# Gates, branches and output projection of the sample tokens in two column halves, the second half moved into the expert stage

## The chip, the cores and the metric

One core of one Trainium2 chip runs the whole program. The engines are PE (TensorE, matrix products), DVE (VectorE), ACT (ScalarE), POOL (GpSimd, here it only issues gathers) and SP (SyncE, here it only issues weight loads). The metric is the device time of one execution in microseconds.

## The reference

Two groups of tokens, 128 prompt tokens and 512 sample tokens, go through two layers (D is 1024). One layer, cut to what matters here:

```python
h = rms_norm(x, norm1) * (1.0 + sc1) + sh1          # shift, scale, gate: silu(cond) @ w_ada
proj = h @ w_in                                     # 3072 gate columns, then the inputs of A, B, C
ya = chunk_gating_mlp(za, ...)                      # branch A
yb = hyena_branch(zb, ...)                          # branch B: long convolution over all tokens
yc = latent_attention(...) @ w_uv                   # branch C: the sample reads all its own keys and the context
ga, gb, gc = split(sigmoid(gates), 3)
merged = ga * (ya @ w_branch_a) + gb * (yb @ w_branch_b) + gc * (yc @ w_branch_c)
x = x + g1 * (merged @ w_out)
h2 = rms_norm(x, norm2) * (1.0 + sc2) + sh2
q = h2 @ peer_wq                                    # 8 heads x 2 x 128
idx, g = the 16 best of 128 * 128 pairs of sub-keys per head     # 8 * 16 = 128 experts a token
a = gelu(dot(peer_u[idx], h2))                      # one row of 1024 per token and expert
x = x + g2 * sum over experts of g * a * peer_v[idx]
```

All four lines from `ga, gb, gc` to `h2` work on each token by itself: they don't mix tokens.

## The kernel before

All data are fp32 with channels on the partitions and tokens along the free axis, so a weight block is the left factor of a matmul and 512 sample tokens are one row of 512 columns. Two tracks share every engine. The **mixing track** does, instance by instance, conditioning (`A`), mixing of the prompt (`P`), queries and key search (`Q`), and mixing of the sample (`S`). The **expert track** goes in slots: one slot is one expert of 128 tokens. In a slot POOL gathers 128 rows of `peer_u` (0.52 MB, line 2182) and 128 rows of `peer_v`; DVE multiplies the u rows with the tokens and sums (`dot_product`, line 2074, a pass over 128x1024). In the prompt's expert stage DVE also adds the v rows to the sum (line 2116), 18 slots later. In the sample's expert stage PE does that: DVE makes a diagonal matrix (line 2149) and PE multiplies it with the v rows, two matmuls of 128x512 a slot (line 1318).

The prompt's expert stage has 174 slots (20 for the choice of experts, 128 dots, and a tail), and the sample's has 512 and a tail (four tiles of 128 tokens). `cuts()` writes a table that says up to which place of the mixing track an engine must have come when it enters a slot, and `weave()` makes each engine's instruction order from it. Every engine runs in that order. `mix_share()` spreads an instance over slots in proportion to `cost()`.

- In the prompt's expert stage the mixing track does the sample's mixing: projections, the inputs of A and B, attention in 16 steps, then 24 gate turns (line 860, left factor from w_in, 8 matmuls of 128x512 each) with 24 branch products (line 860 as well), 8 output turns, norm 2 (line 805). DVE multiplies branch by gate in line 1862 and adds in line 1866; ACT makes the next input `h_s` in line 1383.
- Then the queries of tile 0 run alone up to the first key search, and the sample's expert stage begins.
- In that stage, mixing does the queries of tiles 1 to 3 (slots 17 to 156; PE line 867), next layer's conditioning (157 to 252), prompt mixing (253 to 472) and prompt queries (473 to 508). In the last layer only the final norms are left.

Weights come through SP's queue into a ring of three places of 1 MB, in one fixed order; a load waits until PE has used the load three places back. A gate turn uses half of a 1 MB load (256 of the 3072 gate columns), so a load serves two turns of all 512 tokens. A key search of one turn (`best_keys`, lines 1895 to 1906) is the part of the queries that falls to DVE.

The places that the change touches, in before:

```python
        return [(2 * n, 2 * n + 1) for n in range(4)] if self.sample else [(0,), (1,)]
QUERIES_S = [[Inst("Q", l, True, tiles) for tiles in ((0,), (1, 2, 3))] for l in range(LAYERS)]
                for n in range(4 * two):
                    yield PLACE[i, ("out", n)]
        over(q1, 17, 156)
```

Of the kernel before, what the change touches and what calls it, by code (L numbers as in the profile page):

```python
# [5 lines left out]
ALU = mybir.AluOpType  # L6
# [5 lines left out]
P = 128  # L12
D = 1024
# [54 lines left out]
class Inst:  # L68


    def __init__(self, kind, l, sample=False, tiles=(0,)):
        self.kind, self.l, self.sample, self.tiles = kind, l, sample, tiles
        self.W, self.NT, self.BPT = (SAMPLE, STILES, 1) if self.sample else (PROMPT, 1, 2)
        self.g = 0 if self.sample else 1
# [5 lines left out]
    def gate_groups(self):  # L80

        return [(2 * n, 2 * n + 1) for n in range(4)] if self.sample else [(0,), (1,)]

    def query_turns(self):
# [8 lines left out]
QUERIES_S = [[Inst("Q", l, True, tiles) for tiles in ((0,), (1, 2, 3))] for l in range(LAYERS)]  # L93
# [3 lines left out]
                   for i in [ADAS[l], PROMPTS[l], QUERIES_P[l], SAMPLES[l]] + QUERIES_S[l]] + LASTS  # L97
# [15 lines left out]
def step_turns(m):  # L113
# [15 lines left out]
    return turns  # L129


def turn_order(i):
# [17 lines left out]
    if kind == "Q":  # L150
# [16 lines left out]
        return o  # L167
    s = kind == "S"
# [23 lines left out]
    for group in i.gate_groups():  # L192
        for b in range(3):
            for t in group:
                ring(("gate", b, t))
                if not s:
                    o.append((("gateb", b, t), None))
                ring(("branch", b, t))
    if not s:
        ring(("mt", 0), ("mt", 1))  # L200
    ring(*[("out", n) for n in range(4 * two)], "norm2")
# [3 lines left out]
RING = {"A": (0, 1, 2), "I": (0, 1, 2, 3, 4, 6, 7), "P": (0, 1, 2), "S": (0, 1, 2, 3, 4, 6, 7), "F": (0, 1, 2),  # L205
        "Q": (0, 1, 2)}


def turn_table():

    turns, places, used, at = {}, {}, [0] * 8, 0
    for i in INSTS:
        ring = 0
        for name, bank in turn_order(i):
# [4 lines left out]
            if bank == "ring":  # L219
                bank = RING[i.kind][ring % len(RING[i.kind])]  # L220
                ring += 1
# [8 lines left out]
def bank_uses(last, bank):  # L230

    return max([n + 1 for (i, _), (b, n) in TURN.items() if b == bank and INSTS.index(i) <= INSTS.index(last)],
               default=0)


def chunk_order(i):
# [11 lines left out]
    if i.kind == "Q":  # L248
# [3 lines left out]
        return o  # L252
    take(("QK", 0), ("full", ("qk", i.NT - 1)))
# [13 lines left out]
    for n, group in enumerate(i.gate_groups()):  # L267
        last = group[-1]
        for b in range(3):
            if i.sample:  # L270
                take(("gate", b, n), ("full", ("gate", b, last)))
            else:
                take(("gate", b, n, 0), ("half", ("gate", b, n, 0)))
                take(("gate", b, n, 1), ("full", ("gate", b, last)))
            if b == 0:
                take(("ab", n), ("full", ("branch", 1, last)), 2)
        take(("c", n), ("full", ("branch", 2, last)))
    for n in range(D // CW):
        take(("out", n), ("full", ("out", n * two + two - 1)))
# [6 lines left out]
def chunk_table():  # L286
# [3 lines left out]
    for i in [i for i in INSTS if i.kind in "APSQ"]:  # L290
# [19 lines left out]
def cost(i, name):  # L310
# [3 lines left out]
    if not i.sample and kind in ("gate", "branch"):  # L314
# [6 lines left out]
def mix_share(i):  # L321

    names = [name for name, _ in turn_order(i) if (i, name) in PLACE]
    if i.sample:
# [11 lines left out]
SPREAD = 0.97  # L336
FIRST_SLOT = -PARTS
# [14 lines left out]
def cuts():  # L352
# [3 lines left out]
    for l in range(LAYERS):  # L356
        s, (q0, q1) = SAMPLES[l], QUERIES_S[l]
        for place, share in mix_share(s):
            o.append((slot_of(l, False, min(PROMPT_SLOTS, int(share / SPREAD * PROMPT_SLOTS))), place))
# [10 lines left out]
        over(q1, 17, 156)  # L370
        if l + 1 < LAYERS:
            ada, pr, qp = ADAS[l + 1], PROMPTS[l + 1], QUERIES_P[l + 1]
            over(ada, 157, 252)
            over(pr, 253, 472)
            over(qp, 473, 508)
            end = PLACE[SAMPLES[l + 1], "begin"] - 1
        else:
            for n, i in enumerate(LASTS):
                at = 160 if i.l == STILES else max(184, (i.l + 1) * EXPERTS + M_LAG + 12)
# [68 lines left out]
def build(nc, x_prompt, x_sample, cache_ckv, cache_kpe, c, c_ctx, w_ada, b_ada, norm1, norm2, w_in,  # L448
# [4 lines left out]
    with ExitStack() as ctx:  # L453
# [46 lines left out]
        WORK = 17792  # L500
# [18 lines left out]
        for v, w, n, zc0, kt0, u0, cv0, free, past_keys in ((at_s, SAMPLE, STILES, 0, 2048, 3328, 4352, 7424, PAST),  # L519
# [4 lines left out]
            v.sq2 = view(u0, KC, w)  # L524
            v.hy, v.y_f = view(free, n, 3 * B_W), view(free + n * 768, n, 2 * B_W)
# [9 lines left out]
        v.gate_s, v.gate_y = view(11520, 3, SAMPLE), view(13056, 2, SAMPLE)  # L535
        v.pq_rows, v.pqs, v.rep = view(13184, 2, BANK), view(14208, 2, BANK), view(15232, 4, P)
# [12 lines left out]

        def at(i):  # L550
            return at_s if i.sample else at_p
# [7 lines left out]
        SCRATCH = 896  # L559
        diag = view(9216 + SCRATCH, TOPK, P)  # L560
        y_tok = view(9216 + SCRATCH + TOPK * P, D)
# [81 lines left out]
        merged_ready = signal("merged_ready", P=1, S=1)  # L643
# [15 lines left out]
        def _(sp):  # L659
# [67 lines left out]
            def weights(i):  # L727
# [5 lines left out]
                if i.kind == "Q":  # L733
# [3 lines left out]
                    return  # L737
                for half in range(2):
# [1562 lines left out]
```

## Time and profile before

| what | value |
|---|---|
| median of 3 runs | 4953.66 us (4944.09 to 4954.17) |
| the profiled execution | 4948.02 us |
| its span | 4946.0 us |
| mean granted clock of TensorE | 0.934 |
| busy: PE, DVE, POOL, ACT | 3994.3, 3194.8, 2500.0, 599.3 us |
| moved by DMA | 1579.52 MB, mean 319 GB/s |

The profile is one execution; its time is the span and 2.0 us around it. Stretches below are given by their start and end in the span. In layer 0 the prompt's expert stage with the sample's mixing lies from 342.75 to 1033.6 us (projections and A, B until 535, attention until 696, gates and outputs after that), and the sample's expert stage starts with the dot at 1082.3 us. A row "PE x16" of line 860 counts each fp32 matmul twice, so x16 is one gate turn.

### The profile page before, as it was taken

To read this page: it belongs to the slowest core of one execution; us is meant where nothing else is said; L and a number is where in the kernel's file an instruction comes from. 1 tells how busy PE (TensorE), PEld (TensorE's weight loads), DVE (VectorE), ACT (ScalarE), POOL (GpSimd) and SP (SyncE) were. 2 spreads that over 40 slices of the span, in tenths; PEclk is the share of its full clock that TensorE was granted. 3 is DMA by queue.
4 is the path that set the end of the run, shared out by engine and by line. 5 is a ranking of instruction groups with operands and counts; after the bars stand their busy time and mean duration, and the time that the engine had idled before them with its cause. 6 is when DMAs were issued, how large, how long until landed. Compare 5 with 4: busy or idle time off the path is not lost.

```text
span 4946.0 us, 36846 instructions
## 1 busy us (share of the span) xinstructions
PE 3994.3 (81%) x10767; PEld 1782.0 (36%) x10767; DVE 3194.8 (65%) x7509; ACT 599.3 (12%) x1238; POOL 2500.0 (51%) x2570
## 2 busy tenths in 40 slices
PE   8889789767888886887778888987588777777777
PEld 4554343333333333443333433433233332322223
DVE  0256887647776556765655779774877876676763
ACT  1131330010000001010100314101000100000000
POOL 0002346415665555665555143551366677677774
PEclk9899899888999999999999989998799999999999
DMA  8545779848999999999999366994799999999997
GB/s 275 172 145 193 240 257 335 291 153 319 386 360 376 395 393 367 382 396 386 382 371 360 105 243 220 330 332 139 270 378 376 349 400 409 383 408 387 403 409 299
DMA packets 549494, 1579.52 MB, mean 319 GB/s; under 512 B 51168, under 2 KB 176688, under 8 KB 548018
## 3 DMA queue, kind: packets, MB, share of 16 engines
q0 software_dynamic: 368640, 1342.34, 71.7%
q1 hardware_dynamic: 180082, 234.68, 13.9%
q8 instruction: 90, 1.47, 0.1%
q14 instruction: 106, 0.87, 0.1%
q10 hardware_dynamic: 576, 0.16, 0.0%
HBM read 1574.21 MB, written 2.79 MB: 319 GB/s over the span
## 4 chain that ended last, share of the span: by engine, by line
DMA 34%; PE 22%; DVE 21%; POOL 12%; issue 7%; DVEq 2%; SPq 1%; ACT 1%; PEldq 0%; PEld 0%; ACTq 0%; POOLq 0%
DMA rows<-in_peer_u_dram,idx 30%; POOL rows L2182 10%; DVE rows L2074 8%; PE ps L1318 5%; PE ps L860 5%; PE ps L867 3%; DVE work L2116 3%; DMA rows<-in_peer_v_dram,idx 2%; PE ps L830 2%; POOL work L2182 2%; PE ps L900 1%; SPq L694 1%; DMA work<-in_peer_v_dram,idx 1%; DVEq L1951 1%; DVE work L1898 1%
## 5 line engine op out<-in xcount | busy, mean ns | idle before, releaser
L2182 POOL DMA_INDIRECT rows<-in_peer_u_dram,idx x1280 | 1250.4, 977 | 1526.8 <-DVE dots L2074 654.3
L2074 DVE CUSTOM_DVE_ANT_0 rows<-rows,ps 128x1024 f32<-128x1024 f32 x1024 | 1247.1, 1219 | 884.4 <-DMA rows<-in_peer_u_dram,idx 867.4
L1318 PE MATMUL ps<-rows,work 128*128 128x512 f32 x2736 | 1315.6, 614 | 283.9 <-DMA rows<-in_peer_v_dram,idx 256.5
L2182 POOL DMA_INDIRECT rows<-in_peer_v_dram,idx x940 | 928.0, 987 | 743.2 <-DVE work L2116 394.9
L1318 PEld LDWEIGHTS ps<-rows,work 128*128 128x128 f32 x2736 | 497.5, 194 | 1029.4 <-issue 814.8
L1318 PE MATMUL ps<-work 128*128 128x512 f32 x1360 | 659.2, 614 | 142.9 <-DMA work<-in_peer_v_dram,idx 127.2
L860 PE MATMUL ps<-h_s,ring 128*128 128x512 f32 x1024 | 473.0, 619 | 41.9 <-DVE work L1862 37.7
L1318 PEld LDWEIGHTS ps<-work 128*128 128x128 f32 x1360 | 246.0, 193 | 507.0 <-issue 391.8
L2074 DVE CUSTOM_DVE_ANT_0 rows<-rows,work 128x1024 f32<-128x1024 f32 x256 | 312.1, 1224 | 150.3 <-DMA rows<-in_peer_u_dram,idx 144.9
L2182 POOL DMA_INDIRECT work<-in_peer_v_dram,idx x340 | 320.8, 944 | 147.3 <-issue 87.5
L2149 DVE TENSOR_SCALAR work<-cst,acts,g_w 128x128 f32<-128x128 f32 x1024 | 366.9, 360 | 41.4 <-PE ps L1318 18.6
L2116 DVE SCALAR_TENSOR_TENSOR work<-rows,acts,work 128x1024 f32<-128x1024 f32 x254 | 325.5, 1282 | 15.7 <-DMA rows<-in_peer_v_dram,idx 11.0
L860 PEld LDWEIGHTS ps<-h_s,ring 128*128 128x128 f32 x1024 | 201.4, 199 | 307.5 <-issue 302.7
L860 PE MATMUL ps<-work,ring 128*128 128x512 f32 (+1 forms) x768 | 265.4, 498 | 38.6 <-DVE work L1866 30.4
L867 PE MATMUL ps<-ring,h_s 128*128 128x512 f32 x512 | 237.9, 611 | 21.4 <-ACT h_s L1383 21.4
L860 PEld LDWEIGHTS ps<-work,ring 128*128 128x128 f32 x768 | 128.8, 195 | 169.4 <-issue 123.6
L1630 ACT ACTIVATE acts<-dots 128x16 f32<-128x16 f32 x80 | 17.3, 216 | 1387.8 <-DVEq L2077 1387.7
L867 PE MATMUL ps<-ring,h_p 128*128 128x512 f32 x320 | 153.2, 628 | 23.8 <-DMA ring<-in_w_in_dram 18.0
L830 PE MATMUL ps<-ring,cond_t 128*2 128x256 f32 x768 | 169.8, 379 | 1.3 <-DVE work L1899 1.3
L867 PEld LDWEIGHTS ps<-ring,h_s 128*128 128x128 f32 x512 | 99.4, 197 | 143.2 <-issue 120.1
L1223 PE MATMUL ps<-turned,work 128*128 128x128 f32 x320 | 47.7, 297 | 88.6 <-ACT work L1502 74.2
L2074 DVE DVE_READ_ACCUMULATOR2_ANT dots<- 128x1 f32 x1280 | 105.3, 82 | 0.0
(292 smaller groups left out, 3213.4 us busy)
## 6 DMA issues: line engine op xcount, KB each, us to landing
ring<-in_w_in_dram SPq DMA_DIRECT2D x68, 1024.0 KB, 11.8
ring<-in_w_ada_dram SPq DMA_DIRECT2D x48, 1024.0 KB, 14.2
ring<-in_peer_wq_dram SPq DMA_DIRECT2D x48, 1024.0 KB, 5.2
rows<-in_peer_u_dram,idx POOLq DMA_INDIRECT x1280, 7.3
ring<-in_w_out_dram SPq DMA_DIRECT2D x16, 1024.0 KB, 13.3
rows<-in_peer_v_dram,idx POOLq DMA_INDIRECT x940, 7.3
ring<-in_tables_dram SPq DMA_DIRECT2D x10, 1024.0 KB, 8.0
ring<-in_w_in_dram SPq DMA_DIRECT2D x8, 832.0 KB, 9.3
```

What stands on the lines that cost most here:

```text
L694: sp.dma_start(dst, src).then_inc(params_in, 16)
L830: mm = pe.matmul(a[0:2, 0:CW], cond_t[:, 0:2, k], w[:, k, :], start=k == 0, stop=k == KC - 1)
L860: mm = pe.matmul(a[:, b * i.W:(b + 1) * i.W], w[:, at_w + k, c0 + b * P:c0 + (b + 1) * P], rhs[k], start=k == 0, stop=k == n_rhs - 1)
L867: mm = pe.matmul(a[:, :], lhs[4 * half + k], w[:, k, :], start=half + k == 0, stop=half * k == 3)
L900: mm = pe.matmul(a[:, 0:QK], v.h[:, k, j * P:(j + 1) * P], wqk[k // 4][:, k % 4, :], start=k == 0, stop=k == KC - 1)
L1318: mm = pe.matmul(y_acc[:, cols], diag[:, e % TOPK, :], v_row_of(t, e)[:, cols], start=e == 0, stop=e == EXPERTS - 1)
L1898: dve.match_replace(rep[k], value[:, 0:8], src[k], -3.0e38)
L1951: dve.drain()
L2074: dve.tensor_tensor_reduce(rows[:, s, :], rows[:, s, :], tok, 1.0, 0.0, ALU.mult, ALU.add, dots[:, e:e + 1]).then_inc(rows_u_free, 1)
L2116: ins = dve.scalar_tensor_tensor(y_p, v_row_of(t, e), acts[:, e:e + 1], y_p, ALU.mult, ALU.add)
L2149: dve.tensor_scalar(diag[:, e % TOPK, :], ident, acts[:, e:e + 1], g_w[:, t % 2, e:e + 1], ALU.mult, ALU.mult).then_inc(diag_ready, 1)
L2182: pool.indirect_dma_start(to, None, table, bass.IndirectOffsetOnAxis(ap=idx[:, t % 2, e:e + 1], axis=0)).then_inc(came, 16)
```

## The change

The sample's gates, branches, output projection and norm 2 become instances of their own (`G`), one for tiles 0 and 1 and one for tiles 2 and 3. Each is 256 columns wide and puts two blocks of 128 output channels in one bank, so it has 12 gate turns of 16 matmuls of 128x256 where the whole had 24 turns of 8 matmuls of 128x512; 4 output turns; and a norm of 256 columns. The first (`g0`) stands where all of it stood, at the end of the prompt's expert stage. The second (`g1`) stands in the sample's expert stage at slots 37 to 170, and loads the same weights a second time: per layer 12 loads of 1 MB of w_in, 4 MB of w_out and 4 MB of the branch weights, 20 MiB, that is 20.97 MB. The queries follow the halves: pass `q0` holds tiles 0 and 1 (before only tile 0), pass `q1` tiles 2 and 3 (before 1 to 3). In the prompt's expert stage the sample's mixing is given 0.77 of the slots and `g0` the rest. The rest of the diff makes signal counts follow and gives the second half buffers.

```diff
-QUERIES_S = [[Inst("Q", l, True, tiles) for tiles in ((0,), (1, 2, 3))] for l in range(LAYERS)]
+HALVES = ((0, 1), (2, 3))
+GATES_S = [[Inst("G", l, True, tiles) for tiles in HALVES] for l in range(LAYERS)]
+QUERIES_S = [[Inst("Q", l, True, tiles) for tiles in HALVES] for l in range(LAYERS)]
...
+        if kind == "G":
+
+            self.W, self.NT, self.BPT = len(tiles) * P, len(tiles), 2
...
+def gates_order(i, ring, o):
+    for group in i.gate_groups():
+        for b in range(3):
+            for t in group:
+                ring(("gate", b, t))
+                if not i.sample:
+                    o.append((("gateb", b, t), None))
+                ring(("branch", b, t))
+    if not i.sample:
+        ring(("mt", 0), ("mt", 1))
+    ring(*[("out", n) for n in range(D // CW)], "norm2")
...
+def ring_of(i):
+
+    return (0, 1, 2) if i.kind == "G" and i.first else RING[i.kind]
...
+            if i.sample:
+                take(("gate", b, n), ("full", ("gate", b, last)))
...
+S_SHARE = 0.77
...
-        s, (q0, q1) = SAMPLES[l], QUERIES_S[l]
-        for place, share in mix_share(s):
-            o.append((slot_of(l, False, min(PROMPT_SLOTS, int(share / SPREAD * PROMPT_SLOTS))), place))
+        s, (g0, g1), (q0, q1) = SAMPLES[l], GATES_S[l], QUERIES_S[l]
+        for i, lo, hi in ((s, 0, S_SHARE), (g0, S_SHARE, 1)):
+            for place, share in mix_share(i):
+                share = (lo + share * (hi - lo)) / SPREAD
+                o.append((slot_of(l, False, min(PROMPT_SLOTS, int(share * PROMPT_SLOTS))), place))
...
-        steps = [(FIRST_SLOT, PLACE[q0, ("pqt", 0, 1)]), (FIRST_SLOT + 2, PLACE[q0, ("pqb", 0, 2)]),
-                 (FIRST_SLOT + 4, PLACE[q0, ("key", 0, 1)]), (0, PLACE[q0, ("pqt", 0, 2)]),
-                 (4, PLACE[q0, ("pqb", 0, 3)]), (9, PLACE[q0, ("key", 0, 2)]), (16, PLACE[q0, ("key", 0, 3)])]
+        steps = [(FIRST_SLOT, PLACE[q0, ("pqb", 1, 0)]), (FIRST_SLOT + 2, PLACE[q0, ("pqt", 1, 0)]),
+                 (FIRST_SLOT + 3, PLACE[q0, ("pqb", 0, 1)]), (-1, PLACE[q0, ("key", 0, 1)]),
+                 (6, PLACE[q0, ("pqb", 0, 2)]), (10, PLACE[q0, ("key", 0, 2)]), (20, PLACE[q0, ("pqb", 0, 3)]),
+                 (30, PLACE[q0, ("key", 0, 3)]), (36, PLACE[q0, ("key", 1, 3)])]
...
-        over(q1, 17, 156)
+        over(g1, 37, 170)
+        over(q1, 171, 240)
...
-            over(ada, 157, 252)
-            over(pr, 253, 472)
-            over(qp, 473, 508)
+            over(ada, 241, 316)
+            over(pr, 317, 480)
+            over(qp, 481, 508)
...
+                for i in (PROMPTS[l], QUERIES_P[l], SAMPLES[l], GATES_S[l][0], QUERIES_S[l][0], GATES_S[l][1],
+                          QUERIES_S[l][1]):
                     weights(i)
...
-                for n in range(4 * two):
+                for n in range(D // CW):
...
-                            pe.wait_ge(h_ready.sem, h_ready.after(SAMPLES[l], 2 * KC))
+                                pe.wait_ge(bank_taken[b], bank_uses(GATES_S[l][0], b))
+                        if j % 2 == 0:
+                            pe.wait_ge(h_ready.sem, h_ready.after(GATES_S[l][j // 2], KC))
```

How the order of the instructions changes is shown at three places. On PE at the end of attention (line 1134, the last of branch C) before has a gate turn of 8 and a branch product of 2 or 4 matmuls of 128x512, 24 times:

```order
L1134 MATMUL ps<-work,uv 64x512 x2
L860 MATMUL ps<-h_s,ring 128x512 x8
L860 MATMUL ps<-work,ring 128x512 x2
L860 MATMUL ps<-h_s,ring 128x512 x8
L860 MATMUL ps<-work,ring 128x512 x2
L860 MATMUL ps<-h_s,ring 128x512 x8
```

and the changed kernel, at the same place, where line 860 has become line 927, 12 times:

```order
L1207 MATMUL ps<-work,uv 64x512 x2
L927 MATMUL ps<-h_s,ring 128x256 x16
L927 MATMUL ps<-work,ring 128x256 x4
L927 MATMUL ps<-h_s,ring 128x256 x16
L927 MATMUL ps<-work,ring 128x256 x4
L927 MATMUL ps<-h_s,ring 128x256 x16
```

Each turn keeps its columns in sum (8 x 512 and 16 x 256); there are half as many turns here, and each needs a load of its own. The other half of them stands on PE in the sample's expert stage. There before has the expert's matmuls (line 1318) with the query matmuls (line 867, 4 in a piece) between them:

```order
L1318 MATMUL ps<-work 128x512 x4
L1318 MATMUL ps<-rows,work 128x512 x6
L1215 MATMUL ps<-cst,work 128x128 x4
L1318 MATMUL ps<-rows,work 128x512 x2
L867 MATMUL ps<-ring,h_s 128x512 x4
```

and the changed kernel (line 1318 is now 1393) a little later in that stage:

```order
L927 MATMUL ps<-h_s,ring 128x256 x16
L1393 MATMUL ps<-work 128x512 x4
L1393 MATMUL ps<-rows,work 128x512 x4
L927 MATMUL ps<-work,ring 128x256 x4
L1393 MATMUL ps<-rows,work 128x512 x4
L1393 MATMUL ps<-work 128x512 x4
L927 MATMUL ps<-h_s,ring 128x256 x16
```

A gate turn of 16 matmuls now stands in one piece between the matmuls of two experts. On DVE, the gate stage of before has three dots (line 2074) and three v sums (line 2116) between two branch products (line 1862), from the first product to the last:

```order
L1862 TENSOR_TENSOR work<-work,ps 128x512
L2074 ISA rows,dots<-rows,work 128x1024
L2074 ISA dots 128x1
L2116 SCALAR_TENSOR_TENSOR work<-rows,acts,work 128x1024
L2074 ISA rows,dots<-rows,work 128x1024
L2074 ISA dots 128x1
L2116 SCALAR_TENSOR_TENSOR work<-rows,acts,work 128x1024
L2074 ISA rows,dots<-rows,work 128x1024
L2074 ISA dots 128x1
L2116 SCALAR_TENSOR_TENSOR work<-rows,acts,work 128x1024
L1862 TENSOR_TENSOR work<-work,ps 128x512
```

and the changed kernel (dots in line 2167, v sums in 2209, products in 1954) has this from its third product to its fifth:

```order
L1954 TENSOR_TENSOR work<-work,ps 128x512
L1957 TENSOR_TENSOR work<-work 128x512
L2167 ISA rows,dots<-rows,work 128x1024
L2167 ISA dots 128x1
L2209 SCALAR_TENSOR_TENSOR work<-rows,acts,work 128x1024
L2167 ISA rows,dots<-rows,work 128x1024
L2167 ISA dots 128x1
L2209 SCALAR_TENSOR_TENSOR work<-rows,acts,work 128x1024
L1954 TENSOR_TENSOR work<-work,ps 128x512
L2209 SCALAR_TENSOR_TENSOR work<-rows,acts,work 128x1024 x2
L1954 TENSOR_TENSOR work<-work,ps 128x512
```

After that product there are no dots of the prompt left, only v sums. Counted over the whole order, the first branch product of the sample's gates stands behind 69 dots and 50 v sums of the prompt's 128 in before, and behind 121 dots and 102 v sums in the changed kernel: 52 dots and 52 v sums have moved ahead of the gates, 31 of each ahead of the first softmax step of attention and 21 into attention.

## Rows read from the trace of the kernel before

**Rows 1.** The page: the chain that ended last, by engine.

```profile
DMA 34%; PE 22%; DVE 21%; POOL 12%; issue 7%; DVEq 2%; SPq 1%; ACT 1%; PEldq 0%; PEld 0%; ACTq 0%; POOLq 0%
```

**Rows 2.** Windows, prompt's stage: us; PE, PEld, DVE, ACT, POOL busy; clock; DMA share; GB/s.

```profile
342.75:535.00 192.25, 170.30 (x458) 83.93 (x458) 136.39 (x282) 33.85 (x66) 57.85 (x51) 0.89 0.57 199
535.00:696.00 161.00, 134.10 (x443) 64.92 (x441) 142.31 (x279) 76.15 (x226) 64.46 (x66) 0.91 0.65 210
696.00:1033.60 337.60, 297.94 (x665) 128.69 (x664) 212.26 (x268) 33.36 (x49) 158.48 (x140) 0.94 0.81 284
```

**Rows 3.** Same view, sample's expert stage of layer 0, then of layer 1.

```profile
1185.50:1590.80 405.30, 343.83 (x896) 151.77 (x896) 292.68 (x888) 27.13 (x46) 256.08 (x271) 0.96 0.97 372
1590.80:1825.80 235.00, 195.17 (x568) 71.89 (x568) 127.90 (x287) 12.63 (x29) 131.77 (x141) 1.00 1.04 395
3982.50:4166.30 183.80, 138.68 (x309) 51.00 (x308) 130.58 (x295) 11.90 (x18) 133.47 (x141) 1.00 1.02 407
```

**Rows 4.** PE's timeline, gate stage: start, us, line, what, count, idle before.

```profile
696.00 7.13 PE L860 MATMUL ps<-h_s,ring 128*128 128x512 f32 x16
...
809.52 7.11 PE L860 MATMUL ps<-h_s,ring 128*128 128x512 f32 x16
...
999.10 27.63 PE L860 MATMUL ps<-work,ring 128*128 128x512 f32 x64
...
1044.32 9.80 PE L867 MATMUL ps<-ring,h_s 128*128 128x512 f32 x16 [10.72 <-ACT h_s L1383]
```

**Rows 5.** DMA from 696 to 1033.6: loads, KB each, median us to landing.

```profile
ring<-in_w_in_dram SPq DMA_DIRECT2D x10, 1024.0 KB, 14.1
...
ring<-in_peer_wq_dram SPq DMA_DIRECT2D x3, 1024.0 KB, 5.0
```

**Rows 6.** PE's timeline in the projections: one turn of 256 columns.

```profile
350.31 3.62 PE L908 MATMUL ps<-ring,h_s 128*128 128x256 f32 x16
```

**Rows 7.** DVE's timeline in attention: one dot, one v sum, the next step.

```profile
548.76 1.23 DVE L2074 CUSTOM_DVE_ANT_0 rows<-rows,work 128x1024 f32<-128x1024 f32 x1
...
549.91 1.28 DVE L2116 SCALAR_TENSOR_TENSOR work<-rows,acts,work 128x1024 f32<-128x1024 f32 x1
551.28 0.16 DVE L1937 TENSOR_TENSOR stat<-stat 128x1 f32<-128x1 f32 x1
```

**Rows 8.** DVE by line, 340 to 1050: busy, mean ns, idle before, releaser.

```profile
L1789 DVE TENSOR_SCALAR work<-ps,par 128x512 f32<-128x512 f32 x6 | 4.9, 809 | 8.3 <-PE ps L860 8.3
...
L1818 DVE TENSOR_TENSOR work<-work 128x256 f32<-128x256 f32 x4 | 1.7, 426 | 9.8 <-ACT work L1454 9.4 <-issue 0.5
...
L1810 DVE TENSOR_TENSOR work<-work,ps 128x512 f32<-128x512 f32 x2 | 1.4, 689 | 10.2 <-PE ps L939 10.2
```

**Rows 9.** Same columns, dots alone: 340 to 535, 535 to 696, 696 to 1034.

```profile
L2074 DVE CUSTOM_DVE_ANT_0 rows<-rows,work 128x1024 f32<-128x1024 f32 x31 | 37.3, 1222 | 10.3 <-DMA rows<-in_peer_u_dram,idx 9.2 <-issue 0.2
...
L2074 DVE CUSTOM_DVE_ANT_0 rows<-rows,work 128x1024 f32<-128x1024 f32 x34 | 41.6, 1222 | 1.5 <-DMA rows<-in_peer_u_dram,idx 1.1 <-issue 0.3
...
L2074 DVE CUSTOM_DVE_ANT_0 rows<-rows,work 128x1024 f32<-128x1024 f32 x63 | 77.3, 1226 | 63.4 <-DMA rows<-in_peer_u_dram,idx 62.2
```

**Rows 10.** DVE's timeline, start of the sample's expert stage: one key search.

```profile
1083.44 0.89 DVE L1895 MAX8 work<-ps 128x8 f32<-128x128 f32 x4
...
1088.93 1.22 DVE L2074 CUSTOM_DVE_ANT_0 rows<-rows,ps 128x1024 f32<-128x1024 f32 x1
```

**Rows 11.** DMA queues, packets, MB: 1590.8 to 1825.8, then 3982.5 to 4166.3.

```profile
q0 software_dynamic: 20266, 73.80, 80.6%
q1 hardware_dynamic: 18952, 18.89, 22.9%
...
q0 software_dynamic: 20206, 73.59, 100.8%
q1 hardware_dynamic: 288, 1.05, 1.4%
```

**Rows 12.** PE's timeline in the sample's expert stage: three experts' matmuls.

```profile
2154.10 5.31 PE L1318 MATMUL ps<-rows,work 128*128 128x512 f32 x12
```

More of the change, by code:

```diff
@@ L80, in gate_groups, with nth_norm @@
     def gate_groups(self):
-        return [(2 * n, 2 * n + 1) for n in range(4)] if self.sample else [(0,), (1,)]
+        return [(n,) for n in range(4 if self.sample else 2)]
+    def nth_norm(self, which):
+        return 0 if self.kind == "G" else which
     def query_turns(self):
@@ L191, in turn_order @@
         ring(*[(name, c) for name in "qKSTV" for c in range(2)], ("Y", 0))
[L192 to L198, printed above, removed]
     if not s:
-        ring(("mt", 0), ("mt", 1))
-    ring(*[("out", n) for n in range(4 * two)], "norm2")
-    return o
-RING = {"A": (0, 1, 2), "I": (0, 1, 2, 3, 4, 6, 7), "P": (0, 1, 2), "S": (0, 1, 2, 3, 4, 6, 7), "F": (0, 1, 2),
-        "Q": (0, 1, 2)}
+        gates_order(i, ring, o)
+    return o
+RING = {"A": (0, 1, 2), "I": (0, 1, 2, 3, 4, 6, 7), "P": (0, 1, 2), "S": (0, 1, 2, 3, 4, 6, 7), "G": (0, 1, 2, 3, 4, 6, 7),
+        "F": (0, 1, 2), "Q": (0, 1, 2)}
+def ring_of(i):
+    return (0, 1, 2) if i.kind == "G" and i.first else RING[i.kind]
 def turn_table():
@@ L233, in bank_uses, with gates_chunks @@
                default=0)
+def gates_chunks(i, take):
+    for n, group in enumerate(i.gate_groups()):
+        last = group[-1]
+        for b in range(3):
+            if i.sample:
+                take(("gate", b, n), ("full", ("gate", b, last)))
+            else:
+                take(("gate", b, n, 0), ("half", ("gate", b, n, 0)))
+                take(("gate", b, n, 1), ("full", ("gate", b, last)))
+            if b == 0:
+                take(("ab", n), ("full", ("branch", 1, last)), 2)
+        take(("c", n), ("full", ("branch", 2, last)))
+    for n in range(D // CW):
+        take(("out", n), ("full", ("out", n)))
 def chunk_order(i):
@@ L266, in chunk_order @@
         take("DFT", ("full", ("idft", 0)), 2)
[L267 to L279, printed above, removed]
+        gates_chunks(i, take)
     return o
@@ L313, in cost @@
     w = 4 if i.sample else 2
-    if not i.sample and kind in ("gate", "branch"):
+    if i.kind != "S" and kind in ("gate", "branch"):
         w = {"gate": 2, "branch": 4}[kind]
@@ L1274, in mixing @@
                         yield from queries(i)
+                    elif i.kind == "G":
+                        yield from gates(i)
                     else:
@@ L1465, in mix @@
                     a = full(i, ("gate", b, t))
-                    if r >= 3:
-                        act.wait_ge(*taken_at(i, ("branch",) + slots[r - 3]))
-                    took(act.activation(v.gate_s[:, r % 3, :], a[:, :], ACT.Sigmoid), i, ("gate", b, t))
+                    ring = len(v.gate_s)
+                    if r >= ring:
+                        act.wait_ge(*taken_at(i, ("branch",) + slots[r - ring]))
+                    took(act.activation(v.gate_s[r % ring], a[:, :], ACT.Sigmoid), i, ("gate", b, t))
                 if not i.sample:
```

137 lines of the change are left out of this document (95 added, 42 removed).

## The prediction

> **What bounds the kernel now.** I read the chain that ended last first: DMA has the largest share, 34%, with PE and DVE at 22 and 21% [rows 1]. No engine binds throughout, so the stretches have to be looked at one by one.
>
> In the prompt's expert stage the DMA is not full: 0.57 and 0.65 of the time up to the end of attention, 0.81 in the gate stage [rows 2]. PE leads in the projections (170.3 of 192.3 us) and in the gate stage (297.9 of 337.6), DVE in attention (142.3 of 161.0). In the sample's expert stage the DMA share is 0.97 to 1.04 at 372 to 407 GB/s [rows 3]: gathers and weights together fill the DMA there, and PE (83 to 85% in layer 0) and DVE wait for rows. So the change takes PE work from a stage that PE sets and gives it, with a second load of the weights, to a stage that the DMA sets. Whether that pays depends on what the weights cost there, and on what happens to the prompt's dots and v sums that now lie under the gates.
>
> **The change part by part, per layer.** I make the sum for one layer and double it: the order is the same in both.
>
> *1. The gate stage halves.* Twelve turns with their branch products take 809.52 − 696.00 = 113.5 us; the output turns run from 999.10 for 27.6 us, and from their end to 1033.6 norm 2 takes 6.9 [rows 4]. That row is the second half of the projection's matmuls (x64 of x128). After: 12 turns of as many columns (113.5), half of the projection (27.6), 3.5 of norm 2, and some 4 for the waits for the last merge and the last output. That is 149 in place of 337.6, **−188**. Late weights could take some of it back: the same loads (five for a group of three turns, four groups, and four of w_out) must now come in half the time. A group of five is used in 28.4 us (113.5 / 4), and a load may start when the one three back has been used, so it has the time of two loads' use, on average 2 × 5.7 = 11.4 us. Landing took 14.1 us in the gate stage and 5.0 right behind it [rows 5]. At 5.0 nothing is late; at 14.1 each of 20 loads is 2.7 late, 54 us. Only 7 dots and 26 v sums stay beside these turns by the order, most of them in the first half, so I take a value near the quiet end: +4.
>
> *2. The prompt's dots and v sums move ahead.* 52 dots and 52 v sums leave the gate stage. A dot with a v sum occupies DVE for 551.28 − 548.76 = 2.52 us in attention [rows 7], so they bring 52 × 2.52 = 131. DVE is at 142 of 161 us in attention, so there they lengthen the stage in full. Ahead of attention DVE idles for 192.3 − 136.4 = 55.9 us [rows 2], and three of its waits there, for PE and ACT, are long enough to take in a dot: 8.3 + 9.8 + 10.2 = 28 [rows 8]. The moved dots wait for their rows in turn: 10.3 / 31 = 0.33 us each ahead of attention (31 of them, 10), 1.5 / 34 each within (21, 1) [rows 9]. Together 131 − 28 + 11 = **+114**. Bounds: all idle time ahead of attention filled and no wait, 131 − 56 = 75; nothing filled and each dot waiting as in the gate stage, 63.4 / 63 = 1.0 us, 183. I take 114, because the nearest rows (same stage, same instructions) give 0.33 and not 1.0.
>
> *3. Norm, h and first queries.* PE waits 10.72 us for the last `h_s` before the queries [rows 4]; ACT and DVE have half the columns to do there: **−5** (bounds 0 and −8).
>
> *4. Two more key searches* fall into the first slots, since q0 has two tiles. One takes 1088.93 − 1083.44 = 5.5 us of DVE [rows 10], ahead of a dot on whose row place the next gather waits. The rest of the stage has two fewer, where dots wait for rows anyway. The start has little to hide them: 11, less 3 for what the rows in flight cover, **+8** (0 to 11).
>
> *5. The weights' second load.* 20.97 MB into a full DMA. The price comes from two stretches with the same gathers, 73.80 and 73.59 MB, one with 18.89 MB of weights in 235.0 us, one with 1.05 MB in 183.8 [rows 3, 11]: 51.2 us / 17.84 MB = 2.87 us a MB, 60 us. By the plain rate of 407 GB/s it is 52. In the query stretch only 372 GB/s are reached; 405.3 us × 372 / 407 = 370, so up to 35 us of the DMA's time are free there, which would leave 25. I take **+55** (25 to 60), nearer the rows that contain weights.
>
> *6. PE within the expert stage.* An expert costs PE 5.31 / 3 = 1.77 us [rows 12], a slot of pure gathers 2.63 (183.8 us for 70 slots: 73.59 MB by 1.05). g1 adds 113.5 + 27.6 = 141 us over 133 slots, 1.06 a slot, with 133 × 2.63 + 55 = 405, 3.04 a slot: PE would be busy 93% of it. DMA stays the bound if PE needs no more than a few waits: **0** (rival A has the other case). ACT's and DVE's part of g1, a dozen products and sums of 512 elements at 0.7 us, lies under dots that wait.
>
> The matmuls get narrower, and here a rule can be weighed against a row. A turn of 256 columns x16 takes 3.62 us, one of 512 x16 7.13 [rows 4, 6]: two narrow ones make 7.24, 1.5% more, 2 us in the 141. The Trainium skill speaks against narrow matmuls: "TensorE: Matmul & The Clock Gate", section "Why this matters for your kernels", asks for all dimensions of at least 512, and its section "Back-to-back issue gap" gives 262 and 518 cycles for 256 and 512 columns, from which I estimate 1.2%, also 2 us. By the rule on size the change should lose much more; the row does not bear that out.
>
> The sum is −188 + 4 + 114 − 5 + 8 + 55 + 0 = −12 a layer, −24 in both. Against the profiled execution's 4948.0 that is 4924; the median of the runs is 5.6 above that execution, and the lowest 3.9 below, so I state 4926.
>
> **The rivals.** Terms 1, 2 and 5 are large and nearly cancel; each rival is one of them coming out at another end. Within 0.2%, some 10 us, a measurement can't tell a change of this kernel from none.
>
> *A. PE can't interleave (slower).* PE runs in order: a gate turn of 7.1 us in one piece delays the matmuls of experts, these free v places late, POOL stands before the v gather, and the u gathers queue behind it. Before, PE did 85% in the query stretch (343.8 of 405.3) and never more in this stage. If 85% is its limit, the g1 stretch takes (133 × 1.77 + 141) / 0.85 = 443 instead of 405, +38, 76 in both layers: 5000. It decides as soon as PE's share passes what waits leave it, that is if a slot takes longer than 3.04 us between slots 37 and 170. Against it: the gate stage shows PE at 88% with the same sort of turns [rows 2]. The same side has late loads of weights in g0 (+50 a layer, 5024) from term 1.
>
> *B. Room in the expert stage (faster still).* The second load costs 25 instead of 55, because it fills the dips of the query stretch: −42 a layer, 4864. For it: 372 GB/s against 407. Against it: the dips come from DVE's key searches and from PE, and weights asked for in fixed order don't wait for a dip.
>
> *C. No change.* The 52 moved pairs find nothing to fill in the projections, where DVE waits for PE in its order: term 2 is 126, and the sum is zero: 4948 on the execution, within 10.
>
> **How the numbers follow.** My sum (4905 to 4938 with small errors) has 0.40, B 0.14, C 0.17, A with late weights 0.29. Point: 4926. The range goes from 4860 to 5000: below it lies half of B's tail, above it about a third of A's, together less than 0.2. Faster by over 0.2%: 0.40 + 0.14 = 0.54; within 0.2%: 0.17; slower: 0.29. The forecast's own range is 4900 to 4940.
>
> **What would show it.** Right, if from the end of attention to the first dot of the sample's stage the time falls by 180 to 195 us a layer, attention and what stands ahead of it grow by 100 to 130, and the sample's expert stage grows by 50 to 75 with 20.97 MB more in q1. Wrong by A, if in slots 37 to 170 PE is above 90% and waits stand on v places or on diagonal matmuls, not on u rows. Wrong by late weights, if in g0 PE waits for `ring<-in_w_in_dram` by tens of us, which it does not do before. Wrong by B, if the expert stage grows by less than 40. What would upset all of it is a cost that no row here has: dots in the projections that push the instructions on which PE waits, and so lengthen PE's stage instead of filling DVE's idle time.

## The result and the profile after

The changed kernel takes 4968.99 us (median of 6 runs), the kernel before 4951.19 in the same runs: ratio 1.0041, interval 1.0028 to 1.0054. It is slower by about 18 us where 22 to 24 us less were forecast. The profiled execution has a span of 4965.6 us, 19.6 longer. Four dots of each trace divide it. DVE's timeline of the kernel before, at the first dot of the prompt and of the sample in layer 0 and then in layer 1:

```profile
395.86 1.22 DVE L2074 CUSTOM_DVE_ANT_0 rows<-rows,work 128x1024 f32<-128x1024 f32 x1 [0.21 <-issue]
...
1082.30 1.22 DVE L2074 CUSTOM_DVE_ANT_0 rows<-rows,ps 128x1024 f32<-128x1024 f32 x1 [5.15 <-DMA rows<-in_peer_u_dram,idx]
...
2802.24 1.23 DVE L2074 CUSTOM_DVE_ANT_0 rows<-rows,work 128x1024 f32<-128x1024 f32 x1 [0.20 <-issue]
...
3489.21 1.22 DVE L2074 CUSTOM_DVE_ANT_0 rows<-rows,ps 128x1024 f32<-128x1024 f32 x1 [5.77 <-DMA rows<-in_peer_u_dram,idx]
```

The same dots of the changed kernel:

```profile
390.58 1.23 DVE L2167 CUSTOM_DVE_ANT_0 rows<-rows,work 128x1024 f32<-128x1024 f32 x1 [0.21 <-issue]
...
1022.34 1.22 DVE L2167 CUSTOM_DVE_ANT_0 rows<-rows,ps 128x1024 f32<-128x1024 f32 x1 [5.27 <-DMA rows<-in_peer_u_dram,idx]
...
2803.37 1.23 DVE L2167 CUSTOM_DVE_ANT_0 rows<-rows,work 128x1024 f32<-128x1024 f32 x1 [0.20 <-issue]
...
3436.13 1.22 DVE L2167 CUSTOM_DVE_ANT_0 rows<-rows,ps 128x1024 f32<-128x1024 f32 x1 [5.25 <-DMA rows<-in_peer_u_dram,idx]
```

The prompt's expert stage goes from 686.4 to 631.8 us and from 687.0 to 632.8: −54.6 and −54.2, where the terms 1 to 3 gave −75. What follows up to the next layer goes from 1719.9 to 1781.0 (+61.1), and in layer 1 up to the end of the span from 1456.8 to 1529.5 (+72.7), where the terms 4 to 6 gave +63. So the first is 20 short in both layers, the second right in one and 10 over in the other.

The windows of the changed kernel, columns as in [rows 2]: projections and A, B; attention; gates to norm 2; then slots 0 to 37 and 37 to 170 of the sample's expert stage:

```profile
348.70:614.57 265.87, 175.84 (x459) 85.35 (x459) 208.16 (x366) 32.41 (x66) 124.79 (x109) 0.78 0.74 262
614.57:825.43 210.86, 154.50 (x441) 74.49 (x440) 189.49 (x339) 79.41 (x230) 120.79 (x106) 0.78 0.77 262
825.43:977.90 152.47, 145.23 (x665) 126.23 (x664) 73.49 (x94) 15.99 (x26) 47.50 (x38) 0.99 0.79 276
...
1022.30:1138.10 115.80, 68.10 (x190) 36.49 (x191) 100.14 (x353) 10.87 (x17) 49.39 (x53) 0.78 0.76 272
1138.10:1563.00 424.90, 384.56 (x1203) 228.32 (x1202) 264.05 (x604) 39.92 (x59) 252.05 (x267) 0.97 0.99 380
```

The gates took 152.5 us, as term 1 had it (149 + 4). Attention ends at 825.4 instead of 696.0, 129.4 later, although the first dot stands 5.3 earlier: here are the 20 us. From the first dot to the first gate turn it takes 134.7 us more, for 114 (in layer 1 135.5). The dots show why; DVE by line in these first three stretches, columns as in [rows 9]:

```profile
L2167 DVE CUSTOM_DVE_ANT_0 rows<-rows,work 128x1024 f32<-128x1024 f32 x62 | 75.4, 1224 | 46.3 <-DMA rows<-in_peer_u_dram,idx 43.1 <-issue 0.5
...
L2167 DVE CUSTOM_DVE_ANT_0 rows<-rows,work 128x1024 f32<-128x1024 f32 x54 | 66.1, 1223 | 6.9 <-DMA rows<-in_peer_u_dram,idx 5.0
...
L2167 DVE CUSTOM_DVE_ANT_0 rows<-rows,work 128x1024 f32<-128x1024 f32 x13 | 16.0, 1230 | 15.6 <-DMA rows<-in_peer_u_dram,idx 15.4
```

Ahead of attention 62 dots wait 46.3 us for u rows, where 31 waited 10.3 [rows 9]. All stretches together have 68.8 us of it, before 75.2: the wait moved with the dots and did not stay behind in the gate stage. POOL's waits in that first stretch (total, times, longest) name who holds the gathers, first of the kernel before, then of the changed one:

```profile
POOL rows L2182 <- DVE work L2116: 22.1, 8, 5.9
...
POOL rows L2275 <- DVE work L2209: 62.8, 26, 5.6
POOL rows L2275 <- DVE dots L2167: 52.4, 5, 43.5
```

26 times, where it was 8, POOL stands before a gather of v rows until a v sum (line 2209; 2116 before) has freed a place. In POOL's timeline the u gather that stood behind such a v gather follows it at once:

```profile
469.07 0.94 POOL L2275 DMA_INDIRECT rows<-in_peer_v_dram,idx  x1 [4.00 <-DVE work L2209]
470.31 0.94 POOL L2275 DMA_INDIRECT rows<-in_peer_u_dram,idx  x1 [0.30 <-issue]
474.44 1.90 POOL L2275 DMA_INDIRECT rows<-in_peer_v_dram,idx  x1 [3.19 <-DVE work L2209]
476.64 0.94 POOL L2275 DMA_INDIRECT rows<-in_peer_u_dram,idx  x1 [0.30 <-issue]
```

The prompt has four places for u rows and four for v rows. Behind the u gather of slot n POOL asks for the v row of n − 16. Its place is free when DVE has summed v row n − 20, which it does 18 slots after that row's dot, in slot n − 2. The u gather of n + 1, whose own place has been free since the dot of slot n − 3, comes after that.

In slots 37 to 170 the chain that ended last has changed its owner. Its shares by line, before (1185.5 to 1590.8) and after (1138.1 to 1563), as the view prints them:

```profile
by line: DMA rows<-in_peer_u_dram,idx 37.2%; POOL rows L2182 12.9%; DVE rows L2074 10.0%; issue 7.6%; PE ps L1318 6.7%; DVE work L1898 2.6%; POOL work L2182 2.6%; DVE work L1906 2.5%; DVE work L1899 2.3%; PE ps L830 1.8%; DMA rows<-in_peer_
```

```profile
by line: PE ps L1393 31.5%; PE ps L927 25.5%; DMA rows<-in_peer_u_dram,idx 19.5%; DMA rows<-in_peer_v_dram,idx 8.3%; DMA work<-in_peer_v_dram,idx 3.9%; POOL rows L2275 2.9%; issue 2.3%; DVE rows L2167 2.0%; ACT h_s L1459 0.9%; PE ps L934 0.
```

57% of it is PE now: the experts' matmuls (1393) and the second half's turns (927). PE is busy 384.6 of 424.9 us, 91%, and the DMA is at 0.99 all the same.

### The profile page after: what moved, and what is told of

Its sections match the earlier page's. It is cut to its first block, busy times and chain, and to the rows that moved or that the text cites. A ratio compares the mean times of both kernels' runs of the same rounds, so it can differ in the third digit from the quotient of the medians.

```text
span 4965.6 us, 39614 instructions
## 1 busy us (share of the span) xinstructions
PE 3999.7 (81%) x12079; PEld 2067.3 (42%) x12079; DVE 3199.5 (64%) x7543; ACT 623.6 (13%) x1286; POOL 2531.8 (51%) x2570
## 4 chain that ended last, share of the span: by engine, by line
PE 32%; DMA 29%; DVE 19%; POOL 9%; issue 5%; DVEq 2%; SPq 1%; ACT 1%; PEldq 0%; PEld 0%; ACTq 0%; POOLq 0%
DMA rows<-in_peer_u_dram,idx 21%; PE ps L1393 13%; PE ps L927 10%; POOL rows L2275 8%; DVE rows L2167 6%; DMA rows<-in_peer_v_dram,idx 3%; PE ps L934 3%; DVE work L2209 3%; PE ps L897 2%; DMA ring<-in_w_in_dram 2%; DMA work<-in_peer_v_dram,idx 1%; DMA ring<-in_w_ada_dram 1%; SPq L753 1%; POOL work L2275 1%; DVE work L1989 1%
## 5 line engine op out<-in xcount | busy, mean ns | idle before, releaser
L1393 PE MATMUL ps<-rows,work 128*128 128x512 f32 x2736 | 1289.3, 608 | 224.6 <-DMA rows<-in_peer_v_dram,idx 198.4
L2275 POOL DMA_INDIRECT rows<-in_peer_v_dram,idx x940 | 960.3, 1022 | 775.1 <-DVE work L2209 341.9
L927 PE MATMUL ps<-h_s,ring 128*128 128x256 f32 (+1 forms) x1792 | 460.8, 416 | 29.6 <-DMA ring<-in_w_in_dram 17.0
L927 PEld LDWEIGHTS ps<-h_s,ring 128*128 128x128 f32 x1792 | 343.7, 193 | 150.3 <-issue 91.2
L927 PE MATMUL ps<-work,ring 128*128 128x256 f32 (+1 forms) x1280 | 263.5, 361 | 3.0 <-DVE work L1957 2.3
L927 PEld LDWEIGHTS ps<-work,ring 128*128 128x128 f32 x1280 | 225.9, 192 | 45.9 <-issue 16.8
L1954 DVE TENSOR_TENSOR work<-work,ps 128x512 f32<-128x512 f32 x60 | 41.0, 684 | 145.3 <-PE ps L1100 72.4
L897 PEld LDWEIGHTS ps<-ring,cond_t 128*2 128x2 f32 x768 | 64.8, 87 | 137.8 <-DMA ring<-in_w_ada_dram 25.6
```

The lines of the kernel that those rows point to most:

```text
L897: mm = pe.matmul(a[0:2, 0:CW], cond_t[:, 0:2, k], w[:, k, :], start=k == 0, stop=k == KC - 1)
L927: mm = pe.matmul(a[:, b * i.W:(b + 1) * i.W], w[:, at_w + k, c0 + b * P:c0 + (b + 1) * P], rhs[k], start=k == 0, stop=k == n_rhs - 1)
L1393: mm = pe.matmul(y_acc[:, cols], diag[:, e % TOPK, :], v_row_of(t, e)[:, cols], start=e == 0, stop=e == EXPERTS - 1)
L1954: took(dve.tensor_tensor(dst, gate, a, ALU.mult), i, ("branch", b, t))
L2275: pool.indirect_dma_start(to, None, table, bass.IndirectOffsetOnAxis(ap=idx[:, t % 2, e:e + 1], axis=0)).then_inc(came, 16)
```

## Experiments

Ratios are to the kernel before in the same runs. "37 to 170" is the time from the dot of slot 37 to that of slot 170, for layers 0 and 1.

**The v gathers one slot later**

```diff
-V_LAG_P = 16
+V_LAG_P = 17
```

> The changed kernel, in the prompt's expert stage with the v gathers one slot later (17 instead of 16 behind the u gathers). POOL works in order; at 16 the v gather waits for a place that a v sum two slots back frees, and the next u gather stands behind it, so u rows are asked for only two slots ahead. Theory (the moved dots wait because of that queue): the dots' wait for u rows ahead of attention falls from 46 us to 20 or less, that stage by 20 to 35 us a layer, the time from 4969 to about 4910 to 4930. Rival (landing time of the gathers in a fuller DMA sets the wait): the wait stays at 40 or more and the time within 10 us of 4969.

Measured: 4933.44 us, ratio 0.9967 (0.9954 to 0.9979), 35 less than the changed kernel. Ahead of attention the dots' wait fell from 46.3 to 24.2 us:

```profile
L2167 DVE CUSTOM_DVE_ANT_0 rows<-rows,work 128x1024 f32<-128x1024 f32 x62 | 75.3, 1223 | 24.2 <-DMA rows<-in_peer_u_dram,idx 20.1 <-issue 0.4
```

and the whole prompt stage from 631.8 to 617.6 and from 632.8 to 616.2. So the queue is a cause, with 14 to 17 us a layer, less than the 20 to 35 expected. (Four kernels below have the changed kernel's prompt stage; it took 631.7 to 639.2 in their profiles, so one profile tells such a difference to some 7 us.) The landing time of the rival did not grow: the u gathers of that stretch in the kernel before, in the changed kernel and here (count, median us to landing):

```profile
rows<-in_peer_u_dram,idx POOLq DMA_INDIRECT x34, 6.5
...
rows<-in_peer_u_dram,idx POOLq DMA_INDIRECT x61, 6.2
...
rows<-in_peer_u_dram,idx POOLq DMA_INDIRECT x63, 6.3
```

The 24.2 us of wait that are left are not told apart.

**The same edit in the kernel before**

> The kernel before with the v gathers one slot later, as in e1. In it half of the prompt's dots lie under the gates, where PE sets the pace and waits for DVE about 20 us by branch products. Theory: little to gain, 5 to 15 us a layer, 4920 to 4945. If the queue held back before as much as the changed kernel (rival), it falls by 20 to 35 a layer, to about 4890 to 4910.

Measured: 4858.23 us, ratio 0.9819 (0.9802 to 0.9835), 90 us less: more than either expectation. Its dots in the gate stage (693 to 993 us), then PE's first gate turn and norm 2, and last norm 2 of the kernel before:

```profile
L2074 DVE CUSTOM_DVE_ANT_0 rows<-rows,work 128x1024 f32<-128x1024 f32 x62 | 75.9, 1224 | 23.6 <-DMA rows<-in_peer_u_dram,idx 20.6
```

```profile
693.02 7.13 PE L860 MATMUL ps<-h_s,ring 128*128 128x512 f32 x16
...
985.69 4.88 PE L805 MATMUL ps<-work,mean_w 128*128 128x512 f32 x11
...
1026.57 7.03 PE L805 MATMUL ps<-work,mean_w 128*128 128x512 f32 x16
```

The dots there wait 23.6 instead of 63.4 us [rows 9], and from the first gate turn to norm 2 it takes 292.7 instead of 1026.57 − 696.00 = 330.6 us. I had taken the gate stage for one that PE sets; 38 us of it were the queue's: a branch product of DVE stands behind the dots, and PE's waits in that stage fell from 39 to 13 us. Against the same edit in the changed kernel (4933), the change costs 75 us.

**The pairs ahead, and nothing else**

```diff
+    if i.kind == "S" and kind in ("gate", "branch", "out", "norm2"):
+        w *= 0.27
```

> The kernel before with the planner's cost of the sample's gates, branches, outputs and norm 2 scaled by 0.27, so that 51 dots and 51 v sums move ahead of the gates as in the changed kernel, and nothing else changes (24 turns of 512 columns, one load). Term 2 by itself: attention ends later by 114 by the prediction, by 129 as in the changed kernel. What the gates then get back is what the pairs had held up there: by the prediction's term 1 nothing more than what PE waits, 0 to 15 of 338; by what the v gathers at 17 gave the kernel before, about 40. Time: 5150 to 5180 by the prediction, 5115 to 5140 by the other.

Measured: 5100.21 us, ratio 1.0290 (1.0273 to 1.0307). PE's first gate turn and norm 2:

```profile
827.57 2.84 PE L862 MATMUL ps<-h_s,ring 128*128 128x512 f32 x6
...
1105.05 5.31 PE L807 MATMUL ps<-work,mean_w 128*128 128x512 f32 x12
```

Attention ends 131.6 later than in the kernel before (from the first dot 135.7, in layer 1 135.5), with one weight load and 512 columns throughout: this is term 2 by itself, and it is as large as in the changed kernel. From first turn to norm 2 it takes 277.5 instead of 330.6, so that the pairs had held the gates up by 53 us. Both expectations had the gates give back too little. The window of the gate stage with norm 2, columns as in [rows 2]:

```profile
827.57:1112.10 284.53, 282.94 (x665) 125.25 (x664) 87.03 (x111) 25.31 (x38) 42.16 (x37) 1.00 0.44 146
```

PE's idle time fell from 39.7 us (337.60 − 297.94) to 1.6, and its busy time by 15. Taken in this order, of the 185 us that the gate stage lost in the changed kernel, 53 are from the pairs' leaving and 132 (284.5 − 152.5) from the halving.

**More pairs beside the gates**

```diff
-S_SHARE = 0.77
+S_SHARE = 0.66
```

> The changed kernel with the sample's mixing given 0.66 instead of 0.77 of the prompt's slots, so that about 19 dots and 19 v sums go back from the stretches ahead of the gates to the gates of the first half, where DVE is busy 73 of 152 us. Theory (the pairs cost 2.5 us each where DVE sets the pace, and lie beside PE's work under the gates): attention ends 45 to 50 us earlier a layer, the gates take 10 to 20 more, the time falls by 55 to 80 to about 4890 to 4915. Rival (under the gates they hold up the branch products and PE waits for them): the gates get longer by as much, the time stays within 10 us of 4969.

Measured: 4910.58 us, ratio 0.9917 (0.99 to 0.9933): the time as expected, both its parts larger. Attention ends 60 us earlier in layer 0 and the gates take 33 longer; the prompt stage takes 601.2 and 604.6, some 29 us a layer less. The gates of the first half had room on DVE.

**Loads of the second half cut to an eighth**

```diff
+                if i.kind == "G" and i.first:
+                    src = src[:, 0:1, :]
```

> The changed kernel with the second half's weight loads cut to an eighth (one of eight blocks of rows is loaded, the others are what the ring held; the sample's tiles 2 and 3 are computed from those, all instructions stay): 2.6 instead of 21.0 MB. By term 5 (the second load is paid at 2.87 us a MB in a full DMA) the sample's expert stage falls by 18.3 x 2.87 = 53 us a layer, to 4863. By rival A (PE's turns between the experts' matmuls set it) it falls by less than 20 a layer, to 4930 or more.

Measured: 4929.89 us, ratio 0.9961 (0.9947 to 0.9975). 37 to 170 falls from 424.9 and 423.1 to 407.3 and 405.8, by 17 and not 53, as rival A had it. The chain there is PE's to 79%:

```profile
by line: PE ps L1397 46.4%; PE ps L931 32.8%; DMA rows<-in_peer_u_dram,idx 3.9%; DMA work<-in_peer_v_dram,idx 3.8%; DMA rows<-in_peer_v_dram,idx 2.3%; POOL rows L2279 2.1%; issue 1.6%; ACT h_s L1463 1.0%; PE ps L876 0.9%; PE ps L938 0.8%; P
```

**Turns of the second half in pieces**

```diff
+        for name, _ in turn_order(g1):
+            place = PLACE[g1, name]
+            at = next(slot for slot, to in steps if to == place)
+            if name[0] in ("gate", "out"):
+                gap = min(1, (at - before) / 4)
+                steps.extend((at - gap * (4 - n), place - (4 - n) / 4) for n in (1, 2, 3))
+            before = at
```

> The changed kernel with each gate and output turn of the second half cut on PE into pieces of 4 matmuls (two of the four pieces of a gate turn still stand together), with an expert's matmuls between the pieces; nothing else moves. In the changed kernel the chain of slots 37 to 170 is 57% PE, and POOL waits 64 us there for places of v rows that PE frees. Theory (it is the lump of 7 us in front of the experts' matmuls): that stretch falls from 424 us by 15 to 30 in each layer, to about 4910 to 4940. Rival (PE's load as such, 385 of 425 us busy, in whatever pieces): less than 8 a layer, 4955 or more.

Measured: 4964.25 us, ratio 1.0021 (1.0011 to 1.0031); 37 to 170 takes 421.0 and 423.1. My theory of the lump fell. The chain shows what happened: the u rows' DMA takes over where PE stood, at nearly the same time.

```profile
by line: DMA rows<-in_peer_u_dram,idx 47.0%; PE ps L1418 17.6%; PE ps L947 7.6%; POOL rows L2300 6.2%; DVE rows L2192 5.2%; issue 4.8%; PE ps L935 1.6%; POOL work L2300 1.6%; DVEq L1980 1.3%; ACT h_s L1484 0.9%; PE ps L954 0.8%; DVE work L2
```

**Few matmuls in the second half**

```diff
-                    for k in range(n_rhs):
+                    for k in (0, n_rhs - 1) if i.kind == "G" and i.first else range(n_rhs):
```

> The changed kernel with only the first and last of the matmuls of each sum in the second half's gates, branches and outputs (the rest of these products is left out, so tiles 2 and 3 get other values; every load, wait, DVE and ACT instruction stays): PE does some 100 us less in slots 37 to 170. Theory (PE sets this stretch, the loads little): it falls from 424 to 370 to 390, 35 to 55 a layer, to about 4870 to 4900. Rival (term 5: the loads set it in a full DMA, 350 + 55): it stays above 405, the time above 4930.

Measured: 4962.22 us, ratio 1.0015 (1.0006 to 1.0025); 37 to 170 takes 417.0 and 419.2, 8 and 4 less: as the rival had it. PE is busy 313 us there instead of 385 (71 less where 100 were expected), 75%, and the DMA is at 1.00:

```profile
1145.00:1563.00 418.00, 313.25 (x795) 147.88 (x794) 265.29 (x604) 39.33 (x58) 252.81 (x268) 0.96 1.00 386
```

**Both cuts**

> The changed kernel with both cuts of the second half at once: an eighth of its loads, and two matmuls of each sum (the rest of these loads and products is left out; tiles 2 and 3 get other values). Alone, the loads gave 17 us of the 424 in slots 37 to 170, the matmuls 6. Theory (two bounds at nearly the same height, the DMA with the loads at about 417 and PE with the matmuls at about 406, so that either alone gives little): together they free the stretch down to 360 to 375, 50 to 65 a layer, about 4840 to 4870. Rival (a third thing holds it, the order of ACT or DVE with their waits for the second half's turns): it stays above 395, the time above 4910.

Measured: 4880.91 us, ratio 0.9858 (0.983 to 0.9885); 37 to 170 takes 382.6 and 381.9. Both together give 42 us where one gave 17 and the other 6. That is what two bounds at nearly one height would do, the DMA with the loads at 417 and PE with the matmuls at 407. But 382 lies above the 360 to 375 expected: by the 2.63 us of a pure gather slot these slots would take 350. The window shows the DMA still busy, at 381 GB/s where pure gathers reached 407 [rows 3]; what holds it there stays open.

```profile
1137.60:1520.20 382.60, 312.34 (x793) 148.75 (x792) 263.78 (x604) 39.32 (x58) 250.48 (x267) 0.95 0.98 381
```

**The edits together**

```diff
-V_LAG_P = 16
+V_LAG_P = 17
...
-S_SHARE = 0.77
+S_SHARE = 0.66
```

and the pieces as above.

> The changed kernel with v gathers at 17, the sample's mixing at 0.66 and the second half's turns in pieces, all three together. If the three act in different places (u rows ahead of the gates, DVE under the gates, PE in the sample's stage) their gains add: 18 + 29 + 15 to 30 a layer below 4969, 4815 to 4845. If the first two are one gain (fewer dots ahead leave less wait to save), 4850 to 4880.

Measured: 4877.60 us, ratio 0.9853 (0.9836 to 0.9869). That is the range of the second case, but not its reason. The first two edits gave 36 and 58 us alone, 94 in sum, and the three together give 91: these two all but add. The prompt stage takes 593.9 and 587.6, 38 and 45 us less, where the two alone make 45 in each layer. What is missing is the third: the pieces give nothing here either (37 to 170: 422.4 and 421.5).

The same with one value changed:

```diff
-S_SHARE = 0.66
+S_SHARE = 0.58
```

> As the one before with the sample's mixing at 0.58, so that about a third of the prompt's slots lie beside the gates. If DVE still has room under the gates, another 15 to 30 us in all below it; if not (DVE needs 2.5 us a pair, some 45 pairs and 15 us of products in 152 us), the gates grow by what attention loses and the time is within 10 us of it.

Measured: 4874.61 us, ratio 0.9846 (0.983 to 0.9863): no difference from the one before that can be measured, which is the second case. In layer 0 attention ends 32 us earlier and the gates take 22 longer.

**Other values in the kernel before**

```diff
-V_LAG_P = 16
+V_LAG_P = 18
```

> The kernel before with the v gathers two slots later (18; 17 gave 4858). If the v place was all that held u rows back, 17 has taken that away and 18 gives the same, 4850 to 4865. If v rows now come late for their sums, 5 to 20 more; if there was still a hold left, 4835 to 4850.

Measured: 4873.60 us, ratio 0.9842 (0.9825 to 0.9858), against 0.9819 of 17: the size of the second case, though the intervals just overlap. Its reason does not show in layer 0's gate stage: the v sums wait 5.3 us there, with 17 it was 8.5. The dots' wait for u rows falls from 23.6 to 7.6, but from the first turn to norm 2 it takes 296.2 us, no less than the 292.7 of 17. So 18 brings nothing over 17, and the wait that was left was no longer the stage's bound.

And with 17, the pairs moved the other way:

```diff
-V_LAG_P = 16
+V_LAG_P = 17
...
+    if i.kind == "S" and kind in ("gate", "branch", "out", "norm2"):
+        w *= 1.4
```

> The kernel before with the v gathers at 17 and the planner's cost of the sample's gates, branches, outputs and norm 2 scaled by 1.4, which moves 14 dots and 14 v sums from ahead of the gates to beside them. Theory (a pair costs 2.5 us where DVE sets the pace, and less under the gates, where DVE has some 80 us free): 35 us a layer less ahead of the gates, 10 to 25 more in them, 4810 to 4840 against 4858 without. Rival (the gates are full by now, their products wait behind the dots): 4850 or more.

Measured: 4914.42 us, ratio 0.9921 (0.9908 to 0.9935). The rival was right: attention ends only 12 us earlier than in the kernel with 17 alone (24 by the first dot, which comes 12 later), and from the first turn to norm 2 it takes 30 us longer. PE waits 32 us there for DVE's products and sums, with 17 alone 8. With 512 columns and 76 dots beside them the gates are full.

The best of all is the kernel before with the v gathers at 17: 4858 us, below both kernels.

## Why the prediction was wrong

**The step that failed is term 2**, the moved dots and v sums: +114 a layer, measured 134.7 and 135.5 from the first dot to the first gate turn (129 by position in layer 0), and 135.7 and 135.5 with the pairs moved alone. Its count (31 and 21 pairs of 2.52 us) held: attention has 20 dots more and grew by 210.9 − 161.0 = 50 us, 2.5 each. Its filling held too: DVE's idle time ahead of attention other than for dots fell from 45.6 (55.9 − 10.3) to 11.4 (265.9 − 208.2 − 46.3), by 34 where I had 28. What was wrong is the sentence "I take 114, because the nearest rows (same stage, same instructions) give 0.33 and not 1.0". Those 31 dots had only 12 v sums among them. The moved ones come with a v gather each, behind which the u gathers queue, and their wait grew by 36.0 us for 31 dots, 1.16 each: the row of the gate stage (1.0), which I kept only for the bound, was the like one. Ahead of attention, +36 of waits and −34 of filling cancel, and a pair costs its whole 2.5 us. With 5.4 more of waits in attention the parts make 131 − 34 + 36 + 5 = 138 for the 135 measured. Rival C came nearer (126, nothing gained), but its reason was wrong: the pairs did fill DVE's waits.

**Term 1** was right in size, 185 for 184, but I took all of it for the halving: 53 of it belong to the pairs and went along with them. That is why a halved gate stage paid less than its length. The late loads cost little: PE waited for them three times, 2.9 us at most and 6.1 in all.

**Terms 3 and 4**: −5 against 44.4 − 48.7 = −4.3, and +8 against 115.8 − 103.2 = +12.6 in slots 0 to 37 (layer 1: +12.2).

**Terms 5 and 6**, +55 and 0: from slot 37 on it is 61.1 − 12.6 = +48.5 in layer 0 and some +60 in layer 1 (with term 4, these are the 10 by which layer 1 is over), so the sum fits, by luck: its reason does not. I priced the weights at 2.87 us a MB in a full DMA and let PE go free at 93%. The loads' own price, with most of PE's turns out of the way, is (417.0 − 382.6) / 18.3 MB = 1.9, and the matmuls left out cost, with the loads out of the way, 407.3 − 382.6 = 25 us. My sign of rival A, PE above 90%, was there (91%, and 57% of the chain), but not A's price: PE did more than the 85% that A allowed it. A gave 443 us for this stretch, I 405, and it took 425.

With the v gathers at 17 in both kernels most of the miss in term 2 is gone. The first dot and the first gate turn, in the changed kernel and then in the kernel before (its gate turn, at 693.02, is shown above):

```profile
392.01 1.23 DVE L2167 CUSTOM_DVE_ANT_0 rows<-rows,work 128x1024 f32<-128x1024 f32 x1 [0.21 <-issue]
...
806.26 7.17 PE L927 MATMUL ps<-h_s,ring 128*128 128x256 f32 x32
...
399.86 1.23 DVE L2074 CUSTOM_DVE_ANT_0 rows<-rows,work 128x1024 f32<-128x1024 f32 x1 [0.21 <-issue]
```

That is 414.2 against 293.2 us, 121 more (119 in layer 1; 113 by position), where it was 135. So of the 21 us by which term 2 fell short, 14 to 16 are the queue's, and 5 to 7 stay open. The gates then give back only 141 (299.7 − 158.3), since in the kernel before 38 us of them were gone already, and the change costs 75 us.

## What to carry to other kernels

Before pricing a stage by its busiest engine, look for what the work in it waits on: a stall that belongs to some instructions travels with them, and the stage that they leave looks better than the change made it. For the wait of an instruction that is moved, take the row in which it stands with the same neighbours in its queues, not the nearest in time. A queue that serves two kinds of transfer in order looks ahead only as far as the kind whose places come free last.

## What the runs showed of the hardware

The same matmuls took longer where PE waited more: the granted clock went from 0.89 and 0.91 of 2.4 GHz [rows 2] to 0.78 in the two stretches up to the end of attention, a mean that mixes the levels of 1.2 and 2.4 GHz. Attention's PE rows grew from 134.1 to 154.5 us, while PE's idle time there grew from 27 to 56. That did not lengthen the stretch: DVE was busy 90% of it, and DVE's added work (47) and longer waits for u rows (5) account for its 50 us more.

PE's busy time was no floor. The gate stage of the kernel before has 297.9 us of it at a granted clock of 0.94 [rows 2]. With the pairs moved ahead the same number of matmul records (665) took 282.9 us at 1.00, and the whole stage 284.5, less than PE's busy time before.

Narrow matmuls cost little that shows: where no wait fell into them, the first half's gate turns of 16 matmuls of 128x256 took 7.07 to 7.17 us, those of 8 of 128x512 7.03 to 7.13 (two of them in [rows 4]): 0.6% more, where the prediction drew 1.5% from its row. One of the narrow turns (x32 is one turn):

```profile
889.17 7.07 PE L927 MATMUL ps<-h_s,ring 128*128 128x256 f32 x32
```
